# A two-block transformer on one core: the order of the first transfers, and of the first weight chunk's products

## The reference, cut to what matters

```python
hn = x * rsqrt(mean(x * x) + 1e-6) * norm_mix[0]   # by token
v  = hn @ da_w_qkv[:, 2048:3072]                   # 256 x 1024 times 1024 x 1024
```

## Time and profile before

| | |
|---|---|
| median of three runs | 1223.0 us |
| profiled execution | 1226.66 us |
| its span, first to last instruction | 1224.8 us |
| mean granted TensorE clock | 0.997 of full speed |
| TensorE matmul (PE) busy | 1216.0 us, 99% |
| VectorE (DVE) busy | 965.6 us, 79% |
| ScalarE (ACT) busy | 701.7 us, 57% |
| GpSimd (POOL) busy | 77.5 us, 6% |
| memory traffic | 223.70 MB, mean 183 GB/s |

### The profile page before, as it was taken

The page is one execution under the profiler, slowest core; times in us unless marked ns, Lnnn a source line. Parts: engine busy times, 40 slices in busy tenths (PEclk is TensorE's granted clock), DMA queues, the critical chain, the costliest instruction groups (busy, mean ns, idle before and its releaser), DMA issues.

```text
span 1224.8 us, 20310 instructions
## 1 busy us (share of the span) xinstructions
PE 1216.0 (99%) x7638; PEld 1086.4 (89%) x7638; DVE 965.6 (79%) x1325; ACT 701.7 (57%) x1029; POOL 77.5 (6%) x97
## 2 busy tenths in 40 slices
PE   9999999999999999999999999999999999999998
PEld 7999888888988898888899998888888889888886
DVE  6997887766688878777567988999767887899943
ACT  6576655544657665555446446766545776666642
POOL 0001000032000000000000100000300500000000
PEclk9999999999999999999999999999999999999999
DMA  8535587655455457765555666776565634777551
GB/s 300 179 133 138 151 246 224 207 177 200 166 191 170 139 138 212 197 183 189 178 188 170 213 188 197 200 204 191 182 201 155 208 116 129 221 197 198 189 190 50
DMA packets 277586, 223.70 MB, mean 183 GB/s; under 512 B 8360, under 2 KB 264624, under 8 KB 277264
## 3 DMA queue, kind: packets, MB, share of 16 engines
q1 hardware_dynamic: 275200, 214.44, 57.6%
q0 software_dynamic: 1744, 7.78, 1.8%
q10 hardware_dynamic: 576, 0.57, 0.1%
HBM read 221.71 MB, written 1.06 MB: 182 GB/s over the span
## 4 chain that ended last, share of the span: by engine, by line
PE 95%; DVE 2%; ACT 1%; DMA 1%; issue 0%; ACTq 0%; POOLq 0%; POOL 0%
PE ps L1935 36%; PE ps L1941 19%; PE ps L1812 6%; PE ps L1813 6%; PE ps L1814 6%; PE ps L1908 4%; PE ps L1913 2%; PE ps L2185 2%; PE ps L2063 2%; PE ps L2065 2%; PE ps L2064 2%; PE ps L2151 2%; PE ps L2149 2%; PE ps L2150 2%; PE ps L2204 1%; PE ps L2238 1%
## 5 line engine op out<-in xcount | busy, mean ns | idle before, releaser
L1057 DVE TENSOR_TENSOR wlo<-raw,whi 128x2048 fp32r<-128x2048 f32 x187 | 422.5, 2261 | 101.3 <-ACT whi L665 101.1
L665 ACT CAST whi<-raw 128x2048 fp32r<-128x2048 f32 (+1 forms) x203 | 382.1, 1883 | 133.7 <-PE ps L1814 48.6
L1935 PE MATMUL ps<-x,whi 128*128 128x512 f32 x1408 | 337.4, 391 | 0.0
L1935 PEld LDWEIGHTS ps<-x,whi 128*128 128x128 f32 x1408 | 258.1, 188 | 49.3
L1812 PE MATMUL ps<-x,whi 128*128 128x256 f32 x680 | 196.6, 289 | 0.2 <-DVE wlo L1057 0.2
L1813 PE MATMUL ps<-x,whi 128*128 128x256 f32 x680 | 192.2, 283 | 0.0
L1814 PE MATMUL ps<-x,wlo 128*128 128x256 f32 x680 | 192.2, 283 | 0.0
L1941 PEld LDWEIGHTS ps<-x,wlo 128*128 128x128 f32 x1408 | 180.8, 191 | 7.4
L1941 PE MATMUL ps<-x,wlo 128*128 128x256 f32 x1408 | 183.2, 283 | 0.0
L1812 PEld LDWEIGHTS ps<-x,whi 128*128 128x128 f32 x680 | 129.7, 191 | 2.7 <-issue 1.1
L1813 PEld LDWEIGHTS ps<-x,whi 128*128 128x128 f32 x680 | 129.8, 191 | 0.3
(11 more groups left out here) (205 smaller groups left out, 1479.8 us busy)
## 6 DMA issues: line engine op xcount, KB each, us to landing
raw<-in_ffn_w_in SPq DMA_DIRECT2D x88, 512.0 KB, 4.9
raw<-in_ffn_w_gate SPq DMA_DIRECT2D x44, 512.0 KB, 3.9
raw<-in_ffn_w_up SPq DMA_DIRECT2D x44, 512.0 KB, 5.2
raw<-in_ffn_w_out SPq DMA_DIRECT2D x38, 512.0 KB, 4.0
raw<-in_ffn_w_down SPq DMA_DIRECT2D x32, 512.0 KB, 4.4
raw<-in_na_w_qkv SPq DMA_DIRECT2D x24, 512.0 KB, 4.2
raw<-in_od_w_in SPq DMA_DIRECT2D x24, 512.0 KB, 4.6
raw<-in_da_w_qkv SPq DMA_DIRECT2D x22, 512.0 KB, 5.2
```

The lines of the kernel that those rows point to most:

```text
L665: nc.scalar.copy(whi[:, c % RING, 0:n], raw[:, c % RING, 0:n]).then_inc(w_hi, 1)
L1057: nc.vector.tensor_tensor(wlo[:, c % RING, 0:n], raw[:, c % RING, 0:n], whi[:, c % RING, 0:n].bitcast(F32), ALU.subtract).then_inc(w_lo, 1)
L1935: return mm(bank(banks[f]), hi[:, k, cols[f]], x[:, k, :, :].rearrange("p a t -> p (a t)"), start=first, stop=end, skip_group_check=opened ...
```

## The change: what it does

SP now issues x tile 0 first, then quarters 0 and 1, then x tile 1, and only then the rest; ScalarE's queue keeps the gammas alone. Each further transfer waits until an older one has landed: quarter 2 for x tile 0, quarter 3 for quarter 0, x tiles 2 and 3 for quarter 1, the halves of chunk 1 for quarters 2 and 3, x tiles 4 and 5 for tiles 2 and 3, x tiles 6 and 7 for the first half of chunk 1, chunk 2 for its second half. What follows on SP follows behind these waits.

The products of the first chunk run row by row: for row 0, then row 1, hi x hi and low x for half 0, the same for half 1, then the lo weights of both halves. To match, quarter 1 is cast by ScalarE in place of VectorE, and ahead of x tile 1; VectorE makes the low part of x tile 0 ahead of the first subtraction, and that of x tile 1 after the second. `lo_x` is cut in two functions with the same instructions. TensorE's rounds of ones are 9 in place of 14. The counts of `first_hi` grow by one, since one more cast counts there.

```diff
             src, dst = chunk_sources("v0", 0), chunk_slots("v0", 0)
-            for a in range(4):
+
+            def load_first(a):
                 cs = slice((a % 2) * 512, (a % 2 + 1) * 512)
                 sp.dma_start(dst[a // 2][:, :, cs], src[a // 2][:, :, cs]).then_inc(w0_in[a], 16)
+
+            sp.dma_start(h[:, 0, :], x_source(0)[:, 0, :]).then_inc(first_x, 16)
+            load_first(0)
+            load_first(1)
+            sp.dma_start(h[:, 1, :], x_source(0)[:, 1, :]).then_inc(x0_in[0], 16)
+            sp.wait_ge(first_x, 16)
+            load_first(2)
+            sp.wait_ge(w0_in[0], 16)
+            load_first(3)
+            sp.wait_ge(w0_in[1], 16)
             load_x(1)
             src, dst = chunk_sources("v0", 1), chunk_slots("v0", 1)
             for a in range(2):
+                sp.wait_ge(w0_in[2 + a], 16)
                 sp.dma_start(dst[a], src[a]).then_inc(w1_in[a], 16)
+            sp.wait_ge(x0_in[1], 16)
             load_x(2)
+            sp.wait_ge(w1_in[0], 16)
             load_x(3)
+            sp.wait_ge(w1_in[1], 16)
             load_chunk("v0", 2)
...
             nc.scalar.dma_start(gcol[:], w["gammas"]).then_inc(gcol_in, 16)
-            nc.scalar.dma_start(h[:, 0, :], x_source(0)[:, 0, :]).then_inc(first_x, 16)
-            nc.scalar.dma_start(h[:, 1, :], x_source(0)[:, 1, :]).then_inc(x0_in[0], 16)
             ac.wait_ge(ones_ok, 1)
             nc.scalar.copy(sums[:, 0, :], ones[:, 0:TT])
             ac.wait_ge(gcol_in, 16)
-            for k in range(2):
-                if k:
-                    ac.wait_ge(x0_in[0], 16)
-                else:
-                    ac.wait_ge(first_x, 16)
-                nc.scalar.activation(xs[XBUF["mix0"]][:, k, 0, :], h[:, k, :], ACT.Copy,
-                                     scale=gamma("mix0", k)).then_inc(x_hi, 1)
+            ac.wait_ge(first_x, 16)
+            nc.scalar.activation(xs[XBUF["mix0"]][:, 0, 0, :], h[:, 0, :], ACT.Copy,
+                                 scale=gamma("mix0", 0)).then_inc(x_hi, 1)
+            split_first(1)
+            ac.wait_ge(x0_in[0], 16)
+            nc.scalar.activation(xs[XBUF["mix0"]][:, 1, 0, :], h[:, 1, :], ACT.Copy,
+                                 scale=gamma("mix0", 1)).then_inc(x_hi, 1)
             split_first(2)
             split_first(3)
...
             nc.vector.memset(ones[:], 1.0).then_inc(ones_ok, 1)
-            for q in range(2):
-                ve.wait_ge(w0_in[q], 16)
-                nc.vector.tensor_copy(first_piece(whi, q), first_piece(raw, q)
-                                      ).then_inc(piece_hi, 1)
-            for q in range(4):
-                split_first(q)
+            ve.wait_ge(w0_in[0], 16)
+            nc.vector.tensor_copy(first_piece(whi, 0), first_piece(raw, 0)).then_inc(piece_hi, 1)
             ve.wait_ge(gcol_in, 16)
-            lo_x("mix0", 0)
+            lo_x_tile("mix0", 0)
+            split_first(0)
+            split_first(1)
+            lo_x_tile("mix0", 1)
+            split_first(2)
+            split_first(3)
             lo_x("mix0", 1)
...
                 for kk in range(2):
                     pe.wait_ge(x_hi, kk + 1)
                     for n in range(2):
-                        if kk == 0:
-                            pe.wait_ge(piece_hi, n + 1)
-                        elif n == 0:
-                            pe.wait_ge(first_hi, 1)
+                        if (kk, n) == (0, 0):
+                            pe.wait_ge(piece_hi, 1)
+                        elif (kk, n) == (1, 1):
+                            pe.wait_ge(w_hi, 1)
                         else:
-                            pe.wait_ge(w_hi, 1)
+                            pe.wait_ge(first_hi, kk + 1)
                         product(0, hi, kk, n, kk == 0)
-                for kk in range(2):
+                        if n == 0:
+                            x_ready("mix0", kk)
+                        product(1, hi, kk, n, False)
                     for n in range(2):
                         if (kk, n) == (1, 1):
                             pe.wait_ge(w_lo, 1)
                         else:
                             pe.wait_ge(first_lo, 2 * kk + n + 1)
-                        product(0, lo, kk, n, False)
-                for kk in range(2):
-                    x_ready("mix0", kk)
-                    for n in range(2):
-                        ins = product(1, hi, kk, n, False)
+                        ins = product(0, lo, kk, n, False)
                 ins.then_inc(w_used, 1)
...
             pe.wait_ge(ones_ok, 1)
-            for _ in range(14):
+            for _ in range(9):
                 mm(bank(0)[:, 0:P], ones[:], ones[:], start=True, stop=True)
```

More of the change, by code:

```diff
@@ L1071, in split_first @@
             def split_first(q):
-                if q < 2:
-                    ve.wait_ge(piece_hi, q + 1)
+                if q == 0:
+                    ve.wait_ge(piece_hi, 1)
                 elif q in (3, 5):
@@ L1077, in split_first @@
                 else:
-                    ve.wait_ge(first_hi, q // 2)
+                    ve.wait_ge(first_hi, (0, 1, 2, 0, 3)[q])
                 nc.vector.tensor_tensor(first_piece(wlo, q), first_piece(raw, q),
@@ L1088, in split_third @@
                     else:
-                        ve.wait_ge(first_hi, 3)
+                        ve.wait_ge(first_hi, 4)
                     nc.vector.tensor_tensor(slot2(wlo, 2)[:, kk, :], slot2(raw, 2)[:, kk, :],
@@ L1103, in split_p, with lo_x_tile @@
                                         ).then_inc(p_lo, 1)
+            def lo_x_tile(name, k):
+                x = xs[XBUF[name]]
+                ve.wait_ge(x_hi, 8 * NORM[name] + k + 1)
+                nc.vector.scalar_tensor_tensor(
+                    out=x[:, k, 1, :], in0=h[:, k, :], scalar=gamma(name, k),
+                    in1=x[:, k, 0, :].bitcast(F32), op0=ALU.mult, op1=ALU.subtract
+                    ).then_inc(x_lo, 1)
             def lo_x(name, p):
@@ L1115, in lo_x @@
                 for k in range(2 * p, 2 * p + 2):
[L1116 to L1120, removed]
+                    lo_x_tile(name, k)
             def means(name):
```

## The result

The change made the kernel slower: 1226.01 us (median of 14 runs) against 1222.93 (14 runs of the kernel before), a ratio of 1.0027 with a 95% interval of 1.0020 to 1.0034 (the two medians alone give 1.0025). The forecast was 1220.0.

A forecast was written before the change was run, and what follows sets the result against it. TensorE, busy 99% of the span, was taken as the bound. Gains: 4.1 us at the second chunk, less 0.75 at the third, less 0.55 at sum and spread, rounded to 3.0: 1220.0 us, range 1217.8 to 1222.2.

The forecast's parts named there:

- the forecast 4.1 us of the second chunk: Second weight chunk on TensorE: its products start at 12.3 us instead of 16.43, 4.1 us earlier.
- the forecast's own 18.5: Third weight chunk on TensorE: products start at 18.5 us, not 17.75, cutting the gain to 3.4 us.
- The formula: Whole forecast: gain is 19.0 less the landing of the third chunk's second half (2b), at most 4.1 us.
- The landing: Third chunk's second half (2b) on SP's queue: lands at 16.1 us, hardly moved from the kernel before.
- Rival 5: SP's transfers: waits drain the queue, 2b lands at 18, gain 1.0 us, 1222.0 us; chance 7%.
- The reorder and the fewer rounds: First chunk on TensorE: reordered products and five fewer warm-up rounds, costed at nothing.
- Rival 1: TensorE idle before the second chunk: clock lost again, costing 1.9 us; gain 2.2, 1220.8 us; chance 20%.
- a wait behind 30 us: Later part of the kernel: a new wait there would show the forecast wrong; none was expected.
- The sum of squares and the spread: Behind the third chunk: waiting for the sum of squares and spreading 1/rms costs 0.55 us together.
- late transposes: Spread of 1/rms on TensorE: its transposes come some 0.35 us late, part of the 0.55.
- the warm-up ran at full speed: TensorE's warm-up matmuls: granted clock 1.00 throughout, so nine rounds do what fourteen did.
- rival 4: First chunk on TensorE: products start slow, 24 x 0.43 us, gain 1.1, 1221.9 us; chance 3%.

The follow-up runs named there:

- the usual execution: The kernel before, unchanged, profiled once more (its second profile): measured 1222.86 us, the profiled execution 1222.55 us.
- the first profile: The profiled execution of the unchanged kernel before from which the prediction was worked: 1226.66 us.
- the products alone: The changed kernel with the loads of the kernel before (new product order, nine warm-up rounds, no waits): 1222.54 us, ratio 0.9998.
- the first profile with the late tile: The kernel before with x tile 1 moved behind the first half of the second chunk on SP: profiled execution 1225.3 us, ratio 1.0035.
- the waits alone: The kernel before, its queues, product order and 14 warm-up rounds kept, with only the new SP waits added: 1227.23 us, ratio 1.0034.

## Why the prediction was wrong

**The base of the sum.** It was worked from an execution 3.66 us over the median, and the prediction took this as an offset: "3.0 off gives 1223.7 there and 1220.0 for the median". It was no offset. The 3.66 were the late tile and the lost clock, the very things that the forecast 4.1 us of the second chunk consisted of; the usual execution had neither, so there was little to gain. Its third chunk starts at 17.83 as it is; against that the forecast's own 18.5, with 0.55 behind it, is a loss of 1.2 us. So this step alone turns a gain into a loss, and no rival doubted it. The number to doubt stood in the table: a profiled execution 0.3% off runs that agree within 0.1%.

**The third chunk.** Even against the first profile the gain was 0.8 us and not 3.0 (28.04 - 27.27 in the chain, 0.8 in the span). The formula held: 19.0 less the landing of 2b, 18.04, is 0.96. The landing was mis-sized, 16.1 for 18.0. 1b landed at 12.39 and not 11.2, and 2b took 5.24 from its issue where I counted 4.4. 1a came in at 11.1, over the 10.0 taken, so the second chunk started at 13.57 and not 12.3. I read issue-to-landing times from transfers on a nearly idle queue, and then chose below them; a file of dependent transfers pays such a time at each link. Rival 5 had this size (2b at 18, 1222.0) but on the wrong base. Against the usual execution the third chunk starts 2.74 late (20.57 for 17.83): 0.67 that the forecast's 18.5 would have cost as well, and 2.07 from the late landing. With 0.52 behind it (below) that is 3.26, and the spans differ by 3.3.

**What held.** First products at 4.92 (5.0 forecast), first chunk to 10.65 (10.5). The reorder and the fewer rounds cost nothing that shows in the time (the products alone: 0.9998). Rival 1's clock did not fall in the changed kernel's profile, nor was there a wait behind 30 us; of the two of its runs above 1227 there is no profile.

**What fitted by luck.** The sum of squares and the spread cost 0.52, where 0.55 was forecast: from the third chunk's start to the products behind the spread 27.27 - 20.57 = 6.70, where the usual execution takes 24.01 - 17.83 = 6.18 (24.01 is 23.79 + 0.22). But most of the forecast, 0.35, was for late transposes, and these were not late: they come 27.05 - 24.18 = 2.87 behind the end of the sum, in the usual execution 23.79 - 20.89 = 2.90. The 0.52 lies ahead of them: the first product after the idle time takes 0.47 in the chain and not 0.23, and the sum 0.58 and not 0.34.

**The clock.** The prediction said that the warm-up ran at full speed, because PEclk reads 1.00 there. The timeline of TensorE in the second profile of the kernel before speaks against it:

```profile
1.06 2.93 PE L2337 MATMUL ps<-ones 128*128 128x128 f32 x12 [1.06 <-DVE ones L1565]
...
4.00 1.12 PE L2337 MATMUL ps<-ones 128*128 128x128 f32 x8
```

0.24 us each at first, 0.14 later, at one PEclk of 1.00. The durations agree with the rule that the slow clock is the default (the Trainium skill, TensorE: Matmul & The Clock Gate, What's actually happening), which I set aside for the column. It cost nothing in the changed kernel's profile, where the first eight products took 2.10 us and the wait for 1a would have hidden more. In the products alone the slow start seems to reach into the first chunk: its first eight products took 2.83 us, eight later ones 1.98, and its first four took 1.91, near the 2.02 of four at a granted clock of 0.50 and not the 1.17 of four at 1.00. There no wait behind them hides it. So rival 4 may have been right in kind; its size, all 24 products at half rate, no run shows.

**What stays open.** Without waits the changed kernel still takes about 0.9 us more than the two versions that leave an x tile on ScalarE's queue (1223.49 against 1222.54 and 1222.64). SP issues 1a at 4.02 there, and at 3.08 and 3.55 in the two; whether that is all of it was not separated.

## What to carry to other kernels

Before working from a profile, compare the profiled execution's own time with the median: if they differ by as much as the effect in question, profile again, for the difference may lie in the stage that is to be changed. Here the waits for landings ahead of the next transfers brought the first pieces forward (x tile 1 was taken at 5.71, without them at 6.51) and took bytes from the last (2b was taken at 18.04, without them at 15.82); where a later stage has no cover, add up what must have been moved by then. Judge a reorder by the last transfer of the stretch, not by the first.

## What the runs showed of the hardware that was not expected

Idle time alone does not say whether the clock falls: 2.92 us in the changed kernel, 2.50 in the first profile with the late tile and 2.16 in the waits alone left it at 2.4 GHz, while 1.99 in the first profile of the kernel before, 2.54 in a second profile of the late tile and 2.20 before the third chunk, with the first four lines of waits out, cost it. And a column of the granted clock that reads 1.00 from the start need not be true there; the durations of equal instructions tell. Last, a transfer has landed only with the last of its sixteen steps, and that one can be late alone: 1.9 us behind the fifteenth in one profile, 0.1 in the next of the same kernel.
